# A three-block network on one core: tail projections reordered, and the last modulation product moved from TensorE to VectorE

## The reference

```
# each layer: six modulation vectors from the condition c
m = silu(cond) @ w_mod[layer] + b_mod[layer]          # 1024 x 6144 weights
sh1, sc1, gt1, sh2, sc2, gt2 = split(m, 6)
# layer 0, the hybrid mixer (x: tokens, w_in: 1024 x 2832)
p  = x @ w_in       # conv part | z (512) | beta,decay (16) | q (512) | k, v (256)
qb = rope(rms_norm(q, q_norm)); kb = rope(rms_norm(k, k_norm))
o_b = softmax(qb kb^T / 8) v                           # 8 heads, 64 wide, 512 keys
o_a = bidirectional gated delta rule over chunks of 64
y  = [rms_norm(o_a) * silu(z), o_b] @ w_out
h  = h + gt1 * rms_norm(y)
f  = (silu(a @ w_gate) * (a @ w_up)) @ w_down          # feed-forward, hidden 2816
h  = h + gt2 * rms_norm(f)
# layer 1: m from w_mod[1]; a conformer convolution in place of the mixer, then a feed-forward
```

## Time and profile before

| | |
|---|---|
| median of 3 runs | 2674.57 us (2674.56 to 2683.15) |
| span of the profiled execution | 2689.2 us |
| TensorE busy | 2163.9 us, 80% |
| VectorE busy | 599.4 us, 22% |
| ScalarE busy | 343.5 us, 13% |
| GpSimd busy | 97.0 us, 4% |
| read from HBM | 751.83 MB |

### The profile page before, as it was taken

One profiled execution on the slowest core, in us unless ns is written; L12 is line 12 of the kernel. 1 busy time (PEld: TensorE's weight loads), 2 busy tenths in 40 slices (PEclk: granted clock), 3 DMA queues, 4 the chain that ended last, 5 costly groups with the idle time before them and its releaser, 6 DMA issues.

```text
span 2689.2 us, 35584 instructions
## 1 busy us (share of the span) xinstructions
PE 2163.9 (80%) x15740; PEld 1251.1 (47%) x15740; DVE 599.4 (22%) x1143; ACT 343.5 (13%) x692; POOL 97.0 (4%) x116
## 2 busy tenths in 40 slices
PE   5999998555566565666988865587999999999999
PEld 2444574222223232233554432263576885666874
DVE  1112554001011010112322210055434000461000
ACT  2101222000010000011110100031251000132000
POOL 0001000000000000000111100000030000100000
PEclk8999998999999999999999999988899999999999
DMA  8633706999999999999999999953732454323450
GB/s 329 260 127 140 236 10 230 421 425 425 424 424 422 421 425 415 421 407 424 424 424 424 425 424 425 421 185 105 240 127 63 139 178 153 110 79 113 148 204 37
DMA packets 158907, 755.20 MB, mean 281 GB/s; under 512 B 12249, under 2 KB 75737, under 8 KB 102050
## 3 DMA queue, kind: packets, MB, share of 16 engines
q1 hardware_dynamic: 158754, 752.92, 70.6%
HBM read 751.83 MB, written 1.05 MB: 280 GB/s over the span
## 4 chain that ended last, share of the span: by engine, by line
PE 54%; DMA 40%; DVE 3%; ACT 2%; issue 1%; POOL 0%; DVEq 0%; SPq 0%; ACTq 0%; POOLq 0%
DMA ring<-w_up_dram 16%; PE psum L653 11%; DMA ring<-w_gate_dram 11%; DMA ring<-w_down_dram 8%; PE psum L555 8%; PE psum L681 5%; DMA ring<-hyb_w_dram 4%; PE psum L1176 3%; PE psum L467 2%; PE psum L1560 2%; PE psum L1240 2%; PE psum L446 2%; PE psum L1284 2%; PE psum L1382 1%; PE psum L1655 1%; PE psum L1015 1%
## 5 line engine op out<-in xcount | busy, mean ns | idle before, releaser
L1176 PE MATMUL psum<-ring,arena 128*32 128x320 f32 x4096 | 360.4, 469 | 281.0 <-DMA ring<-w_gate_dram 141.9
L1176 PEld LDWEIGHTS psum<-ring,arena 128*32 128x32 f32 x4096 | 112.0, 111 | 440.6 <-DMA ring<-w_up_dram 170.8
L653 PE MATMUL psum<-arena,ring 128*128 128x256 f32 x1408 | 305.5, 380 | 0.0
L1240 PE MATMUL psum<-ring,arena 128*32 128x512 f32 x1344 | 212.0, 606 | 107.3 <-DMA ring<-w_down_dram 107.3
L653 PEld LDWEIGHTS psum<-arena,ring 128*128 128x128 f32 x1408 | 268.5, 191 | 36.6
L555 PE MATMUL psum<-ring,arena 128*128 128x512 f32 x480 | 213.3, 606 | 10.3 <-ACT arena L2760 8.5
L1240 PEld LDWEIGHTS psum<-ring,arena 128*32 128x32 f32 x1344 | 47.4, 109 | 247.2 <-DMA ring<-w_down_dram 171.8
L555 PEld LDWEIGHTS psum<-ring,arena 128*128 128x128 f32 x480 | 92.7, 195 | 128.2 <-issue 128.2
L2337 DVE TENSOR_TENSOR arena<-arena,psum 128x320 f32<-128x320 f32 (+1 forms) x32 | 16.7, 521 | 580.5 <-PE psum L1176 574.6
L681 PE MATMUL psum<-ring,arena 128*128 128x512 f32 x288 | 125.0, 596 | 0.0
L1185 PE MATMUL psum<-ring,arena 128*32 128x64 f32 x2048 | 119.8, 291 | 0.0
(11 more groups left out here) (376 smaller groups left out, 2121.0 us busy)
## 6 DMA issues: line engine op xcount, KB each, us to landing
ring<-w_gate_dram SPq DMA_DIRECT2D x128, 1376.0 KB, 18.1
ring<-w_up_dram SPq DMA_DIRECT2D x128, 1376.0 KB, 18.1
ring<-w_down_dram SPq DMA_DIRECT2D x112, 1536.0 KB, 19.9
ring<-w_mod_dram SPq DMA_DIRECT2D x72, 1024.0 KB, 5.1
ring<-w_ffn_in_dram SPq DMA_DIRECT2D x88, 512.0 KB, 5.1
ring<-w_ffn_out_dram SPq DMA_DIRECT2D x14, 1536.0 KB, 7.4
ring<-w_in_dram SPq DMA_DIRECT2D x16, 1024.0 KB, 5.6
ring<-hyb_w_dram SPq DMA_DIRECT2D x10, 1024.0 KB, 16.8
```

Source lines behind the costliest of these rows:

```text
L653: ins = nc.tensor.matmul(b[:, i * 256:(i + 1) * 256], ws[k // 4][:, k % 4, u, i * P:(i + 1) * P], R(XT + k * 256, 256), start=(k == 0), st ...
L1176: ins = nc.tensor.matmul(banks[u][c][32 * j:32 * j + 32, 0:GMAIN], R(XST + k * HALF + e * CAP, CAP), w3[:, 64 * c:64 * c + 64, QGROUP * j: ...
L1240: ins = nc.tensor.matmul(ybanks[half][32 * c:32 * c + 32, :], stationary, w, start=((half, c) not in begun), stop=(unit >= 36), skip_group ...
```

## The change

It has two parts.

1. The order of the tail projections is q, keys/values, z in place of z, q, keys/values, on TensorE and in the queue of loads. VectorE no longer copies z. ScalarE applies Silu to z straight from PSUM, before it copies the query transposes, in place of a Silu after attention.
2. The 24 modulation pieces leave TensorE's attention and delta rule. Their loads stand between the pairs of the first feed-forward, `WEIGHED[f]` of them for pair f. VectorE multiplies each piece (128 x 2048) by its 128 condition values, one per partition, and adds it to a running sum `MSUM` of 128 x 2048. After pairs 4, 7 and 10 TensorE sums `MSUM` over the partitions with four matmuls per part (`modulation_sum`). The columns are made after the second slot of the product back, in bank 7. The delta rule rotates through 6 PSUM banks in place of 5.

```diff
+        "pick_0": (a >= 0) & (np.arange(32)[None, :] == 0),
...
+        WEIGHED = (2, 2, 2, 2, 3, 3, 2, 3, 3, 2, 0)
+        SUMMED = (4, 7, 10)
+        def weighed_beside(f):
+            first = sum(WEIGHED[0:f])
+            return [divmod(i, KT) for i in range(first, first + WEIGHED[f])]
...
+            def modulation_sum(tag, p, bank):
+                b = next_bank((tag, p), bank)
+                if nth((tag, p)) > 1:
+                    pe.wait_ge(bank_drained[bank_of((tag, p))], nth((tag, p)) - 1)
+                pe.wait_ge(mod_weighed, tally.due(mod_weighed, KT))
+                for j in range(4):
+                    ins = nc.tensor.matmul(b[32 * j:32 * j + 32, :], const("pick_0"), R(MSUM + j * HALF, HALF),
+                                           start=True, stop=True, skip_group_check=True)
+                    if j == 3:
+                        ins.then_inc(bank_filled[bank_of((tag, p))], 1)
...
+            def weighed_slots(f):
+                for p, k in weighed_beside(f):
+                    enlist(("mod2_1", p, k))
+                    freed_by[("mod2_1", p, k)] = (mod_weighed, p * KT + k + 1)
...
+                            if n == 0 and f:
+                                weighed_slots(f - 1)
...
-                if n == 0:
-                    for p in range(3):
-                        modulation_cols("mod2_1", p)
+                    if n == 0 and f in SUMMED:
+                        modulation_sum("mod2_1", SUMMED.index(f), 6)
...
+                    if n == 0 and i == 1:
+                        for p in range(3):
+                            modulation_cols("mod2_1", p, 7)
...
-            project("hyb", "z", range(2), 512)
             project("hyb", "q", range(2), 512)
...
+            project("hyb", "z", range(2), 512)
...
-            attention("gq", 16, scores2, values2, lambda i: modulation_part("mod2_1", i // KT, i % KT, 4 + i // KT))
-            rotating[0] = 5
+            attention("gq", 16, scores2, values2)
+            rotating[0] = 6
...
-                    if d == 0 and lv <= 4:
-                        for k in (2 * lv - 2, 2 * lv - 1):
-                            modulation_part("mod2_1", 2, k, 5)
...
+            def weigh_modulation(p, k):
+                key, total = ("mod2_1", p, k), R(MSUM, 4 * HALF)
+                w, c = slot(slot_of(key))[:, 0:4 * HALF], col("c2")[:, k * 32:k * 32 + 1]
+                if k == 0 and p:
+                    v.wait_ge(bank_filled[bank_of(("mod2_1", p - 1))], nth(("mod2_1", p - 1)))
+                v.wait_ge(slot_loaded[slot_of(key)], count_of[key])
+                if k == 0:
+                    ins = v.tensor_scalar(total, w, c, None, ALU.mult)
+                else:
+                    ins = v.scalar_tensor_tensor(total, w, c, total, ALU.mult, ALU.add)
+                ins.then_inc(mod_weighed, 1)
...
+            a.preload_act_table(ACT.Silu)
+            for t in range(TT):
+                tag = ("hyb", "z", t)
+                a.wait_ge(bank_filled[bank_of(tag)], nth(tag))
+                ins = a.activation(R(ZG + t * HALF, HALF), result(tag), ACT.Silu)
+                ins.then_inc(bank_drained[bank_of(tag)], 1)
...
-            def pair_in(tag, w, second, pairs):
+            def pair_in(tag, w, second, pairs, after=None):
                 for f in range(pairs):
+                    if after and f > 1:
+                        after(f - 2)
...
-            pair_in("ffn0", T["w_ffn_in"][0], FFN, FT // 2)
+            def last_modulation_in(f):
+                for p, k in weighed_beside(f):
+                    mod_in("mod2_1", T["w_mod_2"][1], p, k, k + 1)
+            pair_in("ffn0", T["w_ffn_in"][0], FFN, FT // 2, last_modulation_in)
+            last_modulation_in(FT // 2 - 2)
```

More of the change, by code:

```diff
@@ L194, in program @@
         mod_scale_ready = semaphore("mod_scale_ready")
+        mod_weighed = semaphore("mod_weighed")
         post_gains_loaded = semaphore("post_gains_loaded")
@@ L474, in modulation_part, with modulation_cols @@
                         frees((tag, p, k), (tag, p) if k == KT - 1 else None)
-            def modulation_cols(tag, p):
-                b = next_bank((tag, "cols", p))
+            def modulation_sum(tag, p, bank):
[8 more added lines that the diff above has]
+                        ins.then_inc(bank_filled[bank_of((tag, p))], 1)
+            def modulation_cols(tag, p, bank=None):
+                b = next_bank((tag, "cols", p), bank)
                 if nth((tag, "cols", p)) > 1:
@@ L1543, in _ @@
             scaled_T("x4", "mod2_1", stack_taps)
-            turn[0] = turn[0] % ROTATING
+            turn[0] = 0
             rotating[0] = 8
@@ L1895, in ffn @@
                     v.wait_ge(bank_drained[bank_of((f"ffn{n}", f, 1))], nth((f"ffn{n}", f, 1)))
+                    if n == 0:
+                        for p, k in weighed_beside(f):
+                            weigh_modulation(p, k)
             v.memset(R(MB, MODQ), 0.0).then_inc(mod_bias_zeroed, 1)
@@ L2431, in _ @@
             for t in range(TT):
-                v.wait_ge(bank_filled[bank_of(("hyb", "z", t))], nth(("hyb", "z", t)))
-                ins = v.tensor_copy(R(ZG + t * HALF, HALF), result(("hyb", "z", t)))
-                ins.then_inc(bank_drained[bank_of(("hyb", "z", t))], 1)
-                v.wait_ge(bank_drained[bank_of(("hyb", "z", t))], nth(("hyb", "z", t)))
-            for t in range(TT):
                 v.wait_ge(bank_filled[bank_of(("hyb", "q", t))], nth(("hyb", "q", t)))
@@ L2595, in _ @@
             readout("dlo", [R(E0 + t * HALF, HALF) for t in range(TT)], row("out_norm"),
-                    lambda t: v.wait_ge(delta_gate, tally.due(delta_gate)),
+                    lambda t: v.wait_ge(bank_drained[bank_of(("hyb", "z", t))], nth(("hyb", "z", t))),
                     [R(ZG + t * HALF, HALF) for t in range(TT)], [R(E0 + 1024 + t * HALF, HALF) for t in range(TT)])
@@ L2791, in ffn @@
                     a.wait_ge(bank_drained[bank_of(give_)], nth(give_))
+                    if n == 0 and f in SUMMED:
+                        keep_rows("mod2_1", SUMMED.index(f))
             def keep_rows(tag, p):
@@ L3094, in _ @@
             attention("gq", WP2)
-            keep_rows("mod2_1", 0)
-            keep_rows("mod2_1", 1)
             betas(0)
-            for t in range(TT):
-                z = R(ZG + t * HALF, HALF)
-                a.activation(z, z, ACT.Silu).then_inc(delta_gate, 1)
-                a.wait_ge(delta_gate, tally.gave(delta_gate))
             gate_decays(0, "gsums", "gsums1")
@@ L3168, in _ @@
             alternate(latent_delta(0), latent_delta(1))
-            keep_rows("mod2_1", 2)
             a.preload_act_table(ACT.Sqrt)
@@ L3508, in _ @@
                                         lambda s: s.rearrange("p (k n) -> p k n", k=KT)))
-            proj_in("hyb", T["hyb_w"], 1536, 512, "z")
+            proj_in("hyb", T["hyb_w"], 2064, 512, "q")
             s.wait_ge(x_ready, tally.due(x_ready, 4))
             post_rows(T["g_mix_post"][0], T["g_ffn_post"][0], (WP2, WT2))
-            proj_in("hyb", T["hyb_w"], 2064, 512, "q")
             grouped_in(("hyb", "bkv"))
-            for p in range(3):
-                mod_in("mod2_1", T["w_mod_2"][1], p)
+            proj_in("hyb", T["hyb_w"], 1536, 512, "z")
             for h in (1, 0):
```

4 lines of the change are left out of this document (2 added, 2 removed).

## The result

The changed kernel takes 2700.18 us (median of 20 runs, 2687.31 to 2706.06). The kernel before took 2685.94 us in the 20 runs beside it (2670.14 to 2696.42). The ratio is 1.005, with a 95% interval of 1.0034 to 1.0067: slower by about 0.5%, where 0.55% faster was forecast. The three runs of before that the forecast started from had a median of 2674.57, the low end of what the kernel does. That moved the forecast's base by 11 us, not its difference: a forecast of -14.6 stands against a measured +14.2.

The account below looks back on a forecast made before the run. The last chain was taken as 54% TensorE and 40% transfers, gains coming from TensorE-bound stretches. Terms -29.9 - 6.5 + 15.2 + 6.8 + 3.2 - 3.4 = -14.6 us took 2674.6 to 2660 us, range 2644 to 2676.

Parts of the forecast that it names:

- Projections: Tail projections: q takes z's place, both TensorE gaps are filled, first transposes of attention at 1869.1 us.
- Attention: Attention without pieces: steps of 2.48 us, end at 1909.0 against 1938.93, minus 29.9 us including the earlier start.
- charged the clock 2.5 us: Start of attention: 2.5 us for TensorE at 1.2 GHz behind the 3.8 us wait, bounds 0 and 7.
- the third rival: Attention stays at 1.2 GHz without the pieces, about 32 us less the 2.5 counted: 2690 us, chance 0.09.
- The rule of the Trainium skill: Attention: transposes don't count for the clock as other matmuls do, so a price of 30 us would be due.
- Delta rule: Delta rule: removed pieces save 9.0 us, 1.6 and 0.9 return as waits; minus 6.5, bounds -2 and -9.
- Ring: First feed-forward: late slots of six make TensorE wait 3.8 us before pairs 6, 7, 9 and 10; plus 15.2.
- The clock behind them: First feed-forward: low clock after each of four waits loses 1.7 us; plus 6.8, bounds 0 and 14.
- the sums: First feed-forward: three sums of four matmuls on TensorE, 1.06 us each; plus 3.2.
- the columns: Between feed-forward and product back: columns no longer stand there, saving a 1.69 us wait and as much clock; minus 3.4.
- Weighing: First feed-forward: VectorE takes 2.4 us a piece, bounds 2.1 and 3.0, hidden beside the matmuls; no cost.

Follow-up runs that it names:

- eleven spare products: Changed kernel plus 11 matmuls of x by the identity, result unread, in TensorE's wait before attention's first transposes: 2674.53 us, ratio 0.996 to the kernel before.
- the order alone: Kernel before with only the new order of projections; modulation pieces stay in attention and delta rule, nothing weighed: 2664.48 us, ratio 0.991.
- the kernel with sixteen pieces: Changed kernel with modulation parts one and two (16 pieces) back in attention's steps, third part's 8 pieces weighed, one beside a pair: 2652.66 us, ratio 0.989.
- the kernel with six spare products: Changed kernel plus 6 matmuls of 128x128x512, result unread, in TensorE's wait behind attention's third score: 2672.70 us, ratio 0.995 to the kernel before.
- the banks counted from 2: Changed kernel with `turn[0] = 2` in place of 0 ahead of the conformer: 2699.30 us, ratio 1.005 to the kernel before.
- the kernel with useful pieces in the loop's first half: Changed kernel with modulation part one in attention's first eight steps, parts two and three weighed, two beside each of eight pairs: 2647.26 us, ratio 0.986.
- the kernel with spare products in each step: Changed kernel plus four piece-shaped matmuls on x in each attention step, without transfers: 2685.78 us, ratio 0.999 to the kernel before.

## Why the prediction was wrong, point by point

- **Projections: right.** First scores 12.0 us earlier, first transposes at 1869.88 against 1869.1, a wait of 4.80 against 3.8.
- **Attention: the step that failed.** It read "each result is wanted a step later, so 2.48 holds", and charged the clock 2.5 us "(bounds 0 and 7)". The steps' length was right at 2.4 GHz, as eleven spare products showed, whose attention ended at 1911.97 though its first transposes came 4.7 us later behind the scores than in the changed kernel (11.4 us against 6.8): 1907.3 without that. What failed is the assumption that TensorE, busy without a pause, comes back to 2.4 GHz. It stayed at 1.2 GHz through thirteen full steps, to 1937.81: 28.8 us later than forecast. It came back only in the delta rule, at about 1950 (0.50 from 1943 to 1948, 0.79 from 1948 to 1953). This is the third rival, priced at 30 us and 2690 us and given 0.09. Its "against", that transposes and values had joined when the clock came back before, left out that the pieces were there too: piece-shaped products on x, added to these same steps, brought the clock back, and transposes and values without them did not.
- **The rule of the Trainium skill** (TensorE: Matmul & The Clock Gate, Part 4: PE-mode transpose) said that transposes count less for the clock, and by it the third rival was due. The trace agrees with the price, 28.8 us against 30; the rule alone doesn't say that the same transposes and products keep 2.4 GHz once they have it, as the kernel with eleven spare products shows. Nor does any run separate the transposes from the score and value products, which stood in the same steps and didn't bring the clock back either.
- **Delta rule: right in sign, too small.** -15.0 against -6.5 with bounds of -2 and -9. Three terms make it up. The pieces cost 11.5 us there, not 9.0 less 2.5, since TensorE's "issue" pauses went with them. Another 6.5 (101.7 us before, 95.2 with the order alone) was low clock in the trace of before, of which the forecast counted only the one long pair of pieces: a window from 2002 to 2009 shows 0.51, 3.4 us lost, and one from 1946 to 1960 shows 0.82. Against them stand 3.1 us of low clock that the changed kernel carried over from its attention: 86.75 us for what the kernel with sixteen pieces did in 83.7.
- **Ring: right.** Pairs 6, 7, 9 and 10 and no others; 14.6 us against 15.2, with the missing half issued 1.7 us before the pair's end, as read. The clock behind them cost 4.9 (three stretches of 1.5 to 1.7) against 6.8. With the sums at 3.2 and the columns, gone from this stretch, at -4.0, the parts give 18.7 for the measured 18.5. The columns' 1.5 us in the product back leave 2.5 of gain where 3.4 was forecast.
- **Weighing: right.** 2351 ns against 2.4 us, never waited for.
- **Missed: the bank.** 3.15 us of wait ahead of the conformer, from the line `turn[0] = 0`, which the forecast passed over; 3.3 us over both rows of the table. The dip of the clock there was in the kernel before too.
- **The sum, with the failed step mended by experiment:** the kernel with six spare products is 14.7 us below before, where -14.6 was forecast. The agreement is in part luck. In its trace the stretch from the first projection to the end of attention takes 86.0 us, 29.5 less than before, and 29.9 was forecast; but the delta rule's takes 84.1 us, 17.6 less, and 6.5 was forecast. What it gave beyond the forecast was used up by what the forecast lacked: 2.7 us of wait at the bank, a block that began 3.6 us later, and the scatter of the runs.

Open: which property of the pieces (width, shape, or how closely they follow each other) brings the clock back, and what makes it fall at the start of attention. Open too: why the second of four equal gaps in the feed-forward (3.67 us) left the clock at 1.00. The other traces with these gaps show no fixed place: with eleven spare products the first and the fourth gap (3.62 and 3.71 us) had no dip behind them, with six the second (3.88), and with the banks counted from 2 all four had one.

## What to carry to other kernels

Work taken off TensorE may have been what brings its clock back: before moving wide products out of a loop of narrow ones, look in the windows at which level the loop starts, and price the whole loop at 1.2 GHz as a rival of its own. Wide products just ahead of the loop, idle ones here, were worth 26 us, where taking the pieces out of the loop saves 16; the kernel with useful pieces in the loop's first half was faster still. And when transfers are threaded between others through a ring, count slots between a freeing and its reuse, not bytes: two pieces a pair brought no wait, three brought 3.65 us each time.

## What the runs showed of the hardware that was not expected

- TensorE was busy without a pause for some 68 us (1870 to 1937.8) and stayed at 1.2 GHz. The same instructions stayed at 2.4 GHz for 37 us when they began there. So the level of these steps hung on what went before, not on the steps alone.
- Products of the pieces' shape, added to each of these steps with no transfer under way, brought the clock back within four steps, by about 1881.
- The clock fell at about 1868 while TensorE was busy (0.93 from 1866 to 1868, 0.50 from 1868 to 1870), behind a wait of only 1.53 us, in the kernel with spare products in each step.
- Gaps of the same length did not act alike: of the twenty-four between 3.6 and 4.4 us in six traces of the feed-forward, twenty had a low clock behind them and four (3.62 to 3.88 us) had none.
- A multiply-add on VectorE of 128x2048 numbers takes 2351 ns, of 128x512 it takes 749: four times the width is 3.14 times the time.
